# One decoder layer on one core: first loads, fillers before the experts, list, flag and bias rows moved

## The reference

```python
proj = x @ w_in + b_in          # q, k, v, indexer q/k/weights, conv GLU in, two gates
y_attn = dsa_attention(q, k, v, qi, ki, wi, rel_bias) @ w_o_attn   # 64 keys of each query kept
y_conv = conformer_conv(conv_in, ...) @ w_o_conv
mix = (sigmoid(g_attn) * y_attn + sigmoid(g_conv) * y_conv) @ w_out
x = layer_norm(ALPHA * x + mix)
# 32 experts, 4 to a token; every expert's weights (12 MB) are read
for e in range(32):
    gu = x @ w_gate_up[e] + b_gate_up[e]
    act = (clip(u) + 1) * (g * sigmoid(1.702 * g))      # g, u: halves of gu, clipped at 7
    out += combine[:, e] * (act @ w_down[e] + b_down[e])
h = ALPHA * x + out
x = layer_norm(h + sigmoid(h @ w_ple_gate) * (p @ w_ple_proj))
```

## Time and profile before

| | us |
|---|---|
| median of 3 runs | 1190.86 |
| profiled execution | 1189.8 |
| its span | 1188.0 |
| TensorE busy in it | 1149.8 (97%) |
| VectorE busy | 297.6 (25%) |
| ScalarE busy | 172.5 (15%) |
| HBM traffic over the span | 376 GB/s |

### The profile page before, as it was taken

The page is one execution under the profiler, slowest core; times in us unless marked ns, Lnnn a source line. Parts: engine busy times, 40 slices in busy tenths (PEclk is TensorE's granted clock), DMA queues, the critical chain, the costliest instruction groups (busy, mean ns, idle before and its releaser), DMA issues.

```text
span 1188.0 us, 13689 instructions
## 1 busy us (share of the span) xinstructions
PE 1149.8 (97%) x5606; PEld 578.4 (49%) x5606; DVE 297.6 (25%) x769; ACT 172.5 (15%) x335; POOL 11.5 (1%) x26
## 2 busy tenths in 40 slices
PE   7999999899999999999999899999999999999997
PEld 6888888734343434434344343434344343434346
DVE  0539932611111121211110211111212111111125
ACT  1204130111010111101110110101111011111112
POOL 0020000000000000000000000000000000000000
PEclk9999999999999999999998999999999999999999
DMA  9994466789999999999999999999999999999970
GB/s 325 346 297 142 142 251 245 268 339 428 427 427 428 428 427 427 426 428 428 428 425 426 426 400 429 427 429 426 428 429 425 430 424 430 425 428 426 430 335 36
DMA packets 64887, 448.16 MB, mean 377 GB/s; under 512 B 7120, under 2 KB 36080, under 8 KB 39984
## 3 DMA queue, kind: packets, MB, share of 16 engines
q1 hardware_dynamic: 58352, 440.84, 90.0%
q10 hardware_dynamic: 6464, 6.33, 1.6%
HBM read 444.53 MB, written 2.62 MB: 376 GB/s over the span
## 4 chain that ended last, share of the span: by engine, by line
PE 88%; DVE 4%; DMA 4%; ACT 1%; issue 1%; SPq 0%; DVEq 0%; ACTq 0%
PE bank L388 55%; PE bank L648 10%; PE bank L375 5%; DMA ring<-in_w_gu 3%; PE bank L408 3%; PE bank L777 2%; PE bank L790 2%; PE bank L1076 2%; PE bank L395 2%; PE bank L703 1%; DVE arena L434 1%; PE bank L382 1%; ACT arena L1244 1%; DVE arena L428 1%; DMA ring<-in_w_in 1%
## 5 line engine op out<-in xcount | busy, mean ns | idle before, releaser
L388 PE MATMUL bank<-ring,arena 128*64 128x512 f32 x1712 | 377.3, 594 | 6.5 <-DVE arena L434 4.1
L388 PE MATMUL bank<-arena 128*64 128x512 f32 x1456 | 322.8, 597 | 4.8 <-DVE arena L434 3.9
L388 PEld LDWEIGHTS bank<-ring,arena 128*64 128x64 f32 x1712 | 120.2, 137 | 241.6 <-issue 225.1
L388 PEld LDWEIGHTS bank<-arena 128*64 128x64 f32 x1456 | 101.9, 137 | 208.2 <-issue 193.6
L428 DVE TENSOR_TENSOR arena<-bank,arena 128x512 f32<-128x512 f32 x33 | 22.8, 692 | 612.7 <-PE bank L395 612.7
L648 PE MATMUL bank<-arena,ring 128*128 128x256 f32 x576 | 128.2, 383 | 0.2 <-DMA ring<-in_w_in 0.2
L648 PEld LDWEIGHTS bank<-arena,ring 128*128 128x128 f32 x576 | 109.8, 192 | 17.6 <-issue 2.8
L1244 ACT ACTIVATE arena<-bank 128x512 f32<-128x512 f32 x62 | 37.0, 597 | 397.1 <-PE bank L388 397.1
L375 PEld LDWEIGHTS bank<-sel,arena 128*128 128x128 f32 x512 | 63.0, 200 | 12.0 <-issue 11.4
L408 PE MATMUL bank<-arena 64*128 64x512 f32 x272 | 67.6, 615 | 1.3 <-ACT arena L1247 0.8
L375 PE MATMUL bank<-sel,arena 128*128 128x128 f32 x512 | 66.1, 289 | 0.5 <-DVE sel L461 0.5
(11 more groups left out here) (196 smaller groups left out, 529.1 us busy)
## 6 DMA issues: line engine op xcount, KB each, us to landing
ring<-in_w_gu SPq DMA_DIRECT2D x70, 2048.0 KB, 25.9
arena<-in_w_gu SPq DMA_DIRECT2D x58, 2048.0 KB, 27.4
ring<-in_w_dn SPq DMA_DIRECT2D x35, 2048.0 KB, 25.7
arena<-in_w_dn SPq DMA_DIRECT2D x29, 2048.0 KB, 26.6
ring<-in_w_in SPq DMA_DIRECT2D x19, 1024.0 KB, 12.9
ring<-in_w_out SPq DMA_DIRECT2D x4, 1024.0 KB, 5.4
arena<-in_w_pg SPq DMA_DIRECT2D x2, 2048.0 KB, 44.7
ring<-in_w_oa SPq DMA_DIRECT2D x2, 1024.0 KB, 6.1
```

The source lines that it names most:

```text
L388: mm = pe.matmul(to[half * CAP:(half + 1) * CAP, :], rows, w[:, half * 512:(half + 1) * 512], start=first, stop=last)
```

## The change

- The first chunk and xT are loaded in quarters. The first two tiles are made together, block by block, into two banks; the table's matmul stands behind them. ScalarE evacuates the first two tiles ahead of the table.
- On ScalarE's queue six of the loads go behind the table's store, and the experts' biases, x and p behind the index key's evacuation.
- Five matmuls whose result nobody reads (keep_clock: identity times 256 columns, into bank 0) stand around the last of the router: one behind the last turn, three ahead of the counting, one ahead of the gather.
- TensorE reads expert 0's flag between the two halves of the first gather. The list of further rounds is made inside expert 0, behind its gate and up products, and the rank lies in another bank.
- Load 11 is issued in two halves, behind block 0 and block 1 of expert 0.
- In expert 0 the bias gates' turn and the combine of the bias rows stand behind down; on ScalarE their copy stands behind the sigmoid.

The diff's core:

```diff
-            turn_of[i] += 1
+            turn_of[i] += 2 if n == ES else 1
...
         def load_pair(sp, n, e, c):
+            if n == ES:
+
+                for half in range(2):
+                    at = slice(half * SLOT, (half + 1) * SLOT)
+                    sp.wait_ge(*((chunk_used, 1) if half else (half_used, 1)))
+                    sp.dma_start(slot_of(n)[:, at], pair_source(e, c)[:, at]).then_inc(e_in[slot_no[n]], 16)
+                return
...
-                HK, (what, c0, n) = KD // 2, FRONT[0]
-                for half in range(2):
-                    ks = slice(half * HK, (half + 1) * HK)
-                    rows = slice(half * HK * P, (half + 1) * HK * P)
-                    sp.dma_start(xT_sb[:, ks, :], xT[rows, :].rearrange("(k p) t -> p k t", p=P)).then_inc(xT_in[half], 16)
+                what, c0, n = FRONT[0]
+                for quarter in range(4):
+                    ks = slice(2 * quarter, 2 * quarter + 2)
+                    rows = slice(2 * quarter * P, (2 * quarter + 2) * P)
+                    sp.dma_start(xT_sb[:, ks, :], xT[rows, :].rearrange("(k p) t -> p k t", p=P)
+                                 ).then_inc(xT_in[quarter], 16)
                     sp.dma_start(w_view(0)[:, ks, :], src[what][rows, c0:c0 + n].rearrange("(k p) c -> p k c", p=P)
-                                 ).then_inc(first_in[half], 16)
+                                 ).then_inc(first_in[quarter], 16)
                 for i, (what, c0, n) in enumerate(FRONT):
                     if i == 0:
...
                 for n in range(ES, NG):
-                    sp.wait_ge(*pair_read(last_in[n]))
+                    if n > ES:
+                        sp.wait_ge(*pair_read(last_in[n]))
...
+                for k in range(KD):
+                    if k % 2 == 0:
+                        pe.wait_ge(xT_in[k // 2], 16)
+                        pe.wait_ge(first_in[k // 2], 16)
+                    for j in range(2):
+                        mm = pe.matmul(bank[tiles.n + j][:, 0:S], w_view(0)[:, k, j * P:(j + 1) * P], xT_sb[:, k, :],
+                                       start=(k == 0), stop=(k == KD - 1))
+                        if k == KD - 1:
+                            mm.then_inc(tile_done, 1)
+                tiles.up(2)
+
                 pe.wait_ge(relb_in, 32)
                 pe.wait_ge(relb_copied, 1)
                 pe.matmul(bank[7][:, 0:S + P], relb_copies, oneh_sb[:, :], start=True, stop=True).then_inc(tab_done, 1)
-                two(0)
...
+                def keep_clock(n):
+
+                    for _ in range(n):
+                        pe.matmul(bank[0][:, 0:S], ident, resT[:, 0, :], start=True, stop=True)
+
                 route(1, range(4, 6))
                 turn_res(1, 3)
+                keep_clock(1)
                 route(1, range(6, KD))
+                pe.wait_ge(mask_ready, 1)
+                keep_clock(3)
 
                 pe.wait_ge(mask_ready, 2)
                 pe.matmul(bank[6][:, 0:NE], upper, mask[:, 0, 0:NE], start=True, stop=True)
...
+                keep_clock(1)
 
                 pe.wait_ge(sel_ready, 1)
-                gather(pe, 0, True)
-
+                gather(pe, 0, True, range(4))
+                flag = pe.alloc_register("pe_two_rounds")
+                pe.wait_ge(wide_ready, 2)
+                read_flag(pe, flag, 0)
+                gather(pe, 0, True, range(4, KD))
                 pe.wait_ge(more_ready, 1)
-                pe.matmul(bank[7][0:MORE, 1:2], upper[0:MORE, 0:MORE], need, start=True, stop=True).then_inc(rank_done, 1)
-                pe.wait_ge(more_ready, 2)
-                pe.matmul(bank[6][0:1, 3 * NE:3 * NE + LIST], expert_no, place, start=True, stop=True)
-                pe.matmul(bank[6][0:1, 3 * NE + LIST:3 * NE + LIST + 1], need, ones[0:MORE, 0:1], start=True, stop=True
-                          ).then_inc(list_done, 1)
+                pe.matmul(bank[6][0:MORE, RANK:RANK + 1], upper[0:MORE, 0:MORE], need, start=True, stop=True
+                          ).then_inc(rank_done, 1)
...
+                def list_further():
+
+                    pe.wait_ge(more_ready, 2)
+                    pe.matmul(bank[6][0:1, 3 * NE:3 * NE + LIST], expert_no, place, start=True, stop=True)
+                    pe.matmul(bank[6][0:1, 3 * NE + LIST:3 * NE + LIST + 1], need, ones[0:MORE, 0:1], start=True,
+                              stop=True).then_inc(list_done, 1)
...
+                        if wait_xt and k == 0:
+                            mm.then_inc(half_used, 1)
...
                     use_gate_up(e, q, weights, e == 0)
+                    if e == 0:
+                        list_further()
...
-                    if e == 0:
-                        turn_bias(gate_sum)
-                    before(e)
+                    if e:
+                        before(e)
                     if q == 1 and e < NE - 1:
                         next_gather(e)
                     if e in (PP_E, PP_E + 2):
                         embed(e)
-                    use_down(e, weights)
+                    use_down(e, weights, 3 if e else 2)
+                    if e == 0:
+                        turn_bias(gate_sum)
+                        before(e).then_inc(d_done, 1)
 
...
-                pe.wait_ge(wide_ready, 2)
-                read_flag(pe, flag, 0)
...
+                for j in range(2):
+                    evac(qiT[:, j, :], ACT.Identity, bT_sb[:, j:j + 1])
+                a.wait_ge(tab_done, 1)
+                a.activation(tab_sb, bank[7][:, 0:S + P], ACT.Identity).then_inc(tab_ready, 1)
+                for j in range(2, 4):
+                    evac(qiT[:, j, :], ACT.Identity, bT_sb[:, j:j + 1])
+
+                a.wait_ge(tab_ready, 1)
+                a.dma_start(table.rearrange("(r c) h i -> (c h) r i", c=NC),
+                            tab_sb.unsqueeze(1).to_broadcast([P, P // NC, S + P])).then_inc(tab_out, 16)
                 a.dma_start(vb, b_in[V0:V0 + 512].partition_broadcast(P)).then_inc(late_in, 16)
...
                 a.dma_start(vb, b_in[V0:V0 + 512].partition_broadcast(P)).then_inc(late_in, 16)
...
                     a.activation(kiT[half * 64:half * 64 + 64, :], bank[6][0:64, 0:S], ACT.Identity,
                                  bias=bki_sb[half * 64:half * 64 + 64, :]).then_inc(ki_out, 1)
+                a.dma_start(bgu, bguT.rearrange("p (e f) -> p e f", e=NE)).then_inc(late_in, 16)
+                a.dma_start(x_sb, x.rearrange("(t p) d -> p t d", p=P)).then_inc(x_in, 16)
+                a.dma_start(pT_sb, pT.rearrange("(k p) t -> p k t", p=P)).then_inc(ple_in, 16)
...
-                    if e == 0:
-                        bias_out(gate_sum)
                     read_flag(a, flag, e + 1)
                     sigmoid(a, e, 0, False)
                     next_gathered(e)
                     embedded(e)
+                    if e == 0:
+                        bias_out(gate_sum)
                     a.wait_ge(d_done, 3 * e + 3)
                     rows_from(gate_turned, 2)
...
+                def list_out():
+                    v.wait_ge(list_done, 1)
+                    nc.vector.tensor_copy(more[:, :], bank[6][0:1, 3 * NE:3 * NE + LIST + 1]).then_inc(more_out, 1)
+
                 def one_round(e):
                     next_pair(e)
+                    if e == 0:
+                        list_out()
```

More of the change, by code:

```diff
@@ L215, in program @@
         arrived = [sem(f"slot{i}_arrived") for i in range(NS)]
-        chunk_used = sem("chunk_used")
+        chunk_used, half_used = sem("chunk_used"), sem("half_used")
         small_in, late_in = sem("small_in"), sem("late_in")
-        xT_in, x_in = [sem("xT_in0"), sem("xT_in1")], sem("x_in")
-        first_in = [sem("first_in0"), sem("first_in1")]
+        xT_in, x_in = [sem(f"xT_in{i}") for i in range(4)], sem("x_in")
+        first_in = [sem(f"first_in{i}") for i in range(4)]
         relb_in, relb_copied = sem("relb_in"), sem("relb_copied")
@@ L367, in gate_bank, with gather @@
             return bank[4 * t + j][:, 0:256]
-        def gather(pe, b=4, first=False):
-            for k in range(KD):
+        def gather(pe, b=4, first=False, ks=range(KD)):
+            for k in ks:
                 if first and k % 4 == 0:
@@ L894, in use_gate_up_twice, with use_down @@
                                 mm.then_inc(gu_done, 1)
+                        if e == 0 and k == 0:
+                            mm.then_inc(half_used, 1)
                         if k in (1, 3, 5):
                             mm.then_inc(chunk_used, 1)
-                def use_down(e, weights):
+                def use_down(e, weights, done=3):
                     pe.wait_ge(t_read, e * 2 + 2)
@@ L933, in rows_of @@
                     pe.wait_ge(rows_out, e * 2 + 2)
-                    combine(pe, q, last=last, done=done)
+                    return combine(pe, q, last=last, done=done)
                 def next_gather(e):
@@ L943, in before @@
                         pe.wait_ge(bias_ready, 1)
```

(21 more changed lines are left out.)

22 lines of the change are left out of this document (6 added, 16 removed).

## The result

The changed kernel takes 1196.78 us (median of 6 runs, 1194.72 to 1197.34) against 1190.55 us (6 runs) for the kernel before on the same chip. The ratio is 1.0047, 95% interval 1.0037 to 1.0058: slower by 6.2 us (difference of the medians; 5.6 by the ratio), where 1190.6 us (1187.4 to 1193.0) was forecast. Its profiled execution took 1197.0 us, with a span of 1195.2. Lines have moved by the edit: the products are L396 and the table's store is L1182. One thing of the first part is to be corrected: the expert of two rounds is expert 14 in the kernel's count from 0, not 12. Expert 0's products begin at 239.8 us and its start is at 620.3, and an expert takes 27.1 us, so 14 experts lie between.

A forecast was written before the change was run, and what follows sets the result against it. TensorE, busy 97%, was taken as the bound, its arrival at 705 us setting the time. Terms 1.9 + 2.3 - 2.4 - 1.5 = +0.3 us gave 1190.6 us for the runs, range 1187.4 to 1193.0.

The forecast's parts named there:

- The later loads on the ACT queue. Price: nothing.: ScalarE's six issues behind the table's store hold it some 5 us, covered by TensorE's next pair of tiles: 0.
- The lower end, -1.5: Worst case allowed for moving ScalarE's loads behind the table's store: 1.5 us lost; the other end was 0.
- The bias rows behind down: In expert 0, down starts 0.45 us earlier, but turn, copy and combine then stand uncovered: loss 2.4 us.
- what the hole costs: Expert 0's pause ahead of down, 2.6 us, lowers the clock and down's products pay: loss 1.5 us (0 to 3.0).
- I take 1.9: At the start, first loads in quarters bring the second pair of tiles 1.5 to 2.2 us earlier: gain 1.9.
- 3.6 to 5 us at half speed: At the start, TensorE's estimated slow time, covering 8.3 to 11.5 instructions, before it reaches full speed.
- the last by 10: At the start, each further quarter pair lands about 1.5 us after the one before, the last by 10 us.
- can only help: At the start, the ACT queue's nine loads leave the stretch of the first loads; claimed harmless, no size given.
- Rival 4: At the start, a load's fixed price paid eight times delays the second pair to 20.3: 1196.3 us, chance 0.06.
- Fillers, flag and list, 2.3.: Around the gather before expert 0, fillers hold the clock and flag and list waits shrink: products earlier, gain 2.3 us.
- The halves, 0.: Load 11 in halves starts 1.7 us earlier in expert 0, but this is forgotten at 685 to 710 us: 0.
- What the loads gain or lose before 705 us is forgotten there.: Behind the expert of two rounds, holes mean loads wait for TensorE, so only TensorE's arrival at 705 us counts.

The follow-up runs named there:

- e1: Changed kernel with all nine of ScalarE's loads issued ahead of its first evacuation again: 1192.43 us, ratio to the kernel before 1.0016.
- e7: Changed kernel with ScalarE's nine loads early again and the bias rows ahead of down again: 1188.32 us, ratio to the kernel before 0.9978.
- e2: Changed kernel with the bias rows' turn, copy and combine ahead of down again: 1192.36 us, ratio to the kernel before 1.0018.
- e3: Changed kernel with the old front (halves, table's matmul first, store behind the second tile), ScalarE's loads still late: 1193.0 us, ratio to before 1.0022.
- e9: Changed kernel with one of the six late loads, the router's bias, issued early again: 1193.84 us, ratio to the kernel before 1.0031.
- e10: Kernel before with only expert 0's bias rows (turn, copy, combine) moved behind down: 1195.82 us, ratio to before 1.0045.
- e11: Kernel before with only the new front (quarters, table's matmul behind, store behind the fourth tile), ScalarE's loads early: 1190.23 us, ratio 0.9995.
- e4: Kernel before with only the fillers, flag and list moved: 1189.2 us, ratio to before 0.9994.
- e8: Kernel before with fillers, flag, list and load 11 in halves: 1189.62 us, ratio to before 0.9993.
- e6: Kernel before with seven extra matmuls stalling TensorE ahead of expert 6's products: 1195.83 us, ratio to before 1.0038.
- e5: Changed kernel with seven extra matmuls stalling TensorE ahead of expert 6's products: 1201.08 us, ratio to the kernel before 1.0081.

## Why the prediction was wrong

The sum was 1.9 + 2.3 - 2.4 - 1.5 and 0 for the queue. By its steps:

1. **"The later loads on the ACT queue. Price: nothing."** This step failed, and is worth 4.4 us in the profile (index part, against e1) and 4.0 to 4.4 in the runs (e1 against the changed kernel, e7 against e2). I priced six issues at about 5 us from their early rows and found them covered. Behind the store the fifth of them lasts until the store has nearly landed, 11 to 12 us from the store's issue. The lower end, -1.5, was no bound: the row that I needed was the store's own 11.2 us, as the time for which the queue may be closed. e3 and e9 show that it is the order and the distance behind the store that decide, and not which load.
2. **"The bias rows behind down", with "what the hole costs".** -3.9 was forecast (-2.4 and -1.5), and -5.0 measured in the profile (e10 alone: -5.2, and 4.9 to 5.4 in the runs). Direction and mechanism were right: down paid 1.7 for the clock in the changed kernel and 2.4 in e10 (1.5 forecast), and 3.2 us stand between down and expert 1's products (3.3 forecast).

   What was mis-sized is the stretch from VectorE's sum to down, 4.14 instead of 3.3. I took that from expert 2, as if the chain were the same there. It isn't: in expert 2 ScalarE loads no table (its sigmoid starts at 310.80, 0.10 us behind VectorE's clip of the same tile, L430), while in expert 0 the load of 1.28 us stands ahead of the sigmoid, before and after. My premise that it would begin earlier once the copy was gone brought 0.14 us: 1.45 us behind VectorE's sum before (255.92), 1.31 in the changed kernel (259.74), where the load begins behind its wait for VectorE although ScalarE has been idle for 1.87 us. The Trainium skill says as much (ScalarE: Activation LUTs, Step-by-step, the table-load gate): the load is placed right before the ACTIVATE that needs it. The trace agrees. The same page gives 1.38 us of drain beside the 1.28 us of the load (What ACT_TABLE_LOAD costs). The 1.28 is in the trace, the drain is not: the ACTIVATE starts 0.01 us behind the load.
3. **"I take 1.9" for the quarters.** Measured -1.2 in the changed kernel's profile, and +1.6 to -0.2 in seven others with quarters; e11, the front alone, gains 0.6 us by its medians, which its interval doesn't tell from nothing. On the average of the profiles the second pair begins at 16.1 with quarters and 16.9 with halves (16.3 to 17.4).

   Two things failed. First, "3.6 to 5 us at half speed": the clock came up 9.3 us behind TensorE's first matmul in the changed kernel, 3.2 to 6.2 in the others with quarters and 4.6 to 7.3 in those with halves. What decides it is open. The pause before the second quarter (0.57 us in the changed kernel, 0.37 in e7, where it took 6.2) may have a part in it, which isn't shown: without any pause up to that moment it took anything from 3.2 to 7.3 us. Whether the changed kernel's other executions started as slowly as the profiled one isn't known.

   Second, "the last by 10": the last quarter landed at 11.8 to 13.0 (12.1 in the changed kernel), and the second chunk, which I had as "wanted only near 14.5" without looking at its landing, was not there. In the trace of the kernel before it lands at 14.8, 11.6 us behind its issue, so even a warm TensorE could not have begun the second pair much before 15. That the small loads' leaving "can only help" was right for this chunk, by about 1 us (14.8 to 15.2 with eight or nine of them late, 15.8 to 16.7 with all early), at a price of 4.4 elsewhere.

   Rival 4, a fixed price paid eight times (second pair at 20.3), was wrong too; that its 1196.3 us is near the measured time is chance, since its 3.8 us at the front were 1.2. By the Trainium skill's cost components (DMA: Bandwidth & Descriptors), the eight, one after another, would end near 21 us, an estimate. The page gives them for DMAs that gpsimd issues, and these are issued by SyncE. They had landed by 13.0, so most of such a fixed price overlaps; whether a part doesn't is not shown, because the small loads shared the transfers.
4. **Fillers, flag and list, 2.3.** Right: 2.3 in every profile that has them but e9 (1.8). The list costs 0.41 us in expert 0 (26.75 against 26.34), 0.55 forecast. In the runs this part alone (e4) gives only 0.7 to 1.4 us, with a spread of 4.7; what eats it in some executions is open. Of the forecast's other allowances the flag's, 0.15 us, was short once (e9, 0.69).
5. **The halves, 0.** Right (e8 against e4).
6. **"What the loads gain or lose before 705 us is forgotten there."** True only while there are holes. Where they come to 1.5 us or more, the rest is 504.9 to 506.5 us (nine profiles; e6, at 507.0, is the exception); in the four with less (changed, e2, e7, e10) it is 507.9 to 508.9. The changed kernel's TensorE loses 8.4 us up to expert 1 and wins 4.5 back at expert 14, by luck with its clock, and the loads, which fell back with it, set the end: 3.4 us. That rest and holes go together is shown; that the late loads are the cause is argued from this and the chain, and e5 did not settle it.

The profile's ledger, changed kernel against before: front -1.2, index -4.5, mix +2.3, expert 0 -5.0, expert 1 to expert 15 +4.5 (the expert of two rounds), rest -3.4, together -7.3 us, the difference of the spans. The forecast had +1.9, 0, +2.3 and -3.9 for the first four and nothing for the last two.

## What to carry over

A DMA issue is not a fixed half microsecond (0.34 to 7.20 us on ScalarE here): small loads directly behind the table's store held the engine that issued them nearly until the store landed, so put such loads ahead of the store, or well behind it, or on an engine with nothing due. Work that stands in a pause is free, and the same work moved behind the matmuls that end the pause cost its whole length here and the clock besides. Before a stretch is taken over from another place as a price, see that it holds the same instructions: expert 2 had no table load. Splitting first loads helps only as far as the next load, issued behind all the pieces, isn't what TensorE waits for next.

## What the runs showed of the hardware that I had not expected

- The fifth DMA issued from ScalarE behind a 1.5 MB store (11.1 to 12.9 us to landing) ended 0.7 to 1.2 us before the store landed, in five kernels. In the four where it stood directly behind the store it held ScalarE for 6.65 to 7.20 us, for a 16 KB and an 8 KB load alike; with 7 us between (e3) for 1.62. Early in the kernel nine loads in a row were issued with no hold above 2.28 us. What it is that fills up wasn't tried.
- At the start the windows print a granted clock of 1.00 while instructions take twice their time, because the trace has no record of the clock yet. The first record comes 3.2 us (e9) to 9.3 us (changed) behind TensorE's first matmul: x24 in 5.42 us in e9, 6.43 in e7 and 7.87 in the changed kernel, with the same front.
- The pause at expert 14 lowers the clock in most executions, but not always, and its length doesn't order them: 32 instructions take 3.98 us behind a pause of 1.68 (changed) and 1.74 (e10), but 4.78 behind 1.60 (e5), 5.46 behind 1.72 (e2), 4.76 (e4) and 6.54 (before) behind 1.90, and 7.09 behind 2.40 (e8).
